# Moving eight later-modulation steps from the first linears of a transformer block to the linears beside its attention

## What is computed

```python
sh_l, sc_l, g_l = [m[:, None, :] for m in modulation(c, ada_w[i], ada_b[i])]
...
q_a = (rms_norm(c_q, q_lora_g) @ wq_b).reshape(b, l, A_HEADS, A_NOPE + A_ROPE)
kv_a = (rms_norm(c_kv, kv_lora_g) @ wkv_b).reshape(b, l, A_HEADS, A_NOPE + A_V)
...
lqp, lkp = apply_rope(lqp, ang_a), apply_rope(lkp, ang_a)
...
y_a = block_attention(lq_a, k_a_all, v_a_all, A_SCALE)
y_b = block_attention(lqb.reshape(b, s, B_KV_HEADS, B_GROUP, B_HEAD_DIM), k_b_all, v_b_all, B_SCALE)
```

## Time and profile before

| | us |
|---|---|
| median of 3 runs | 2868.02 (2866.8 to 2870.78) |
| profiled execution | 2862.45 |
| its span, first to last instruction | 2860.7 |
| TensorE matmuls busy | 2746.7 (96%) |
| VectorE busy | 1810.2 (63%) |
| ScalarE busy | 1247.6 (44%) |
| GpSimd busy | 271.8 (10%) |

### The profile page before, as it was taken

The page is one execution under the profiler, slowest core; times in us unless marked ns, Lnnn a source line. Parts: engine busy times, 40 slices in busy tenths (PEclk is TensorE's granted clock), DMA queues, the critical chain, the costliest instruction groups (busy, mean ns, idle before and its releaser), DMA issues.

```text
span 2860.7 us, 50571 instructions
## 1 busy us (share of the span) xinstructions
PE 2746.7 (96%) x22173; PEld 2595.9 (91%) x22173; DVE 1810.2 (63%) x2228; ACT 1247.6 (44%) x1375; POOL 271.8 (10%) x330
## 2 busy tenths in 40 slices
PE   6899999999999999999999999998999999999998
PEld 3598977788988998989999999988999999999998
DVE  2358867788777545556556556696566775467753
ACT  4333444445443344444444437545444444344444
POOL 0022102120111000002122120003000000000000
PEclk9899999999999999999999999999999999999999
DMA  9867535574776555435555553440245555555554
GB/s 375 323 228 259 192 135 193 209 274 171 252 246 228 192 193 176 163 137 188 179 175 175 176 177 138 156 166 16 104 171 196 193 188 191 198 196 195 194 189 140
DMA packets 93036, 546.88 MB, mean 191 GB/s; under 512 B 12657, under 2 KB 12817, under 8 KB 47889
## 3 DMA queue, kind: packets, MB, share of 16 engines
q1 hardware_dynamic: 69552, 466.39, 46.0%
q0 software_dynamic: 20480, 67.13, 7.0%
q10 hardware_dynamic: 2784, 10.15, 0.9%
HBM read 541.51 MB, written 2.10 MB: 190 GB/s over the span
## 4 chain that ended last, share of the span: by engine, by line
PE 67%; DVE 7%; ACT 2%; issue 2%; DMA 0%; DVEq 0%; ACTq 0%
PE bank L733 66%; DVE r L2173 2%; ACT r L1476 1%; DVE f L2743 1%; PE bank L801 1%; DVE f L2210 1%; DVE f L2807 0%; ACT f L1838 0%; DVE f L2804 0%; DVE f L2820 0%; DVE f L2796 0%; DMA f<-in_units 0%; DMA f<-in_later 0%; ACT L1826 0%; DVE f L2555 0%
## 5 line engine op out<-in xcount | busy, mean ns | idle before, releaser
L733 PE MATMUL bank<-r,r 128*128 128x256 f32 (+1 forms) x19596 | 2388.3, 284 | 40.5 <-DVE r L2173 18.3
L733 PEld LDWEIGHTS bank<-r,r 128*128 128x128 f32 x19596 | 2320.6, 189 | 98.8 <-DVE r L2173 25.9
L2173 DVE TENSOR_TENSOR r<-f,r 128x2048 fp32r<-128x2048 f32 (+2 forms) x447 | 961.3, 2152 | 687.2 <-ACT r L1476 685.0
L1476 ACT CAST r<-f 128x2048 fp32r<-128x2048 f32 (+2 forms) x447 | 792.0, 1774 | 850.3 <-PE bank L733 664.5
L733 PE MATMUL bank<-f,f 128*128 128x128 f32 (+9 forms) x1992 | 317.7, 375 | 51.5 <-DMA f<-in_units 23.0
L733 PEld LDWEIGHTS bank<-f,f 128*128 128x128 f32 (+2 forms) x1992 | 214.1, 175 | 111.7 <-issue 50.3
L2210 DVE SCALAR_TENSOR_TENSOR f<-f,f,f 128x512 f32<-128x512 f32 x240 | 179.8, 749 | 52.7 <-DMA f<-in_later 37.1
L3068 POOL DMA_DIRECT2D f<-in_later x256 | 137.5, 537 | 786.8 <-DVE f L2210 469.9
L2743 DVE SCALAR_TENSOR_TENSOR f<-f,f,f 128x255 f32<-128x255 f32 (+1 forms) x272 | 133.7, 494 | 8.8
L1493 ACT COPY f<-bank 128x512 f32<-128x512 f32 x149 | 83.9, 584 | 111.8 <-PE bank L733 106.1
L3077 POOL TENSOR_TENSOR f<-f,f 32x512 f32<-32x512 f32 x24 | 61.7, 2570 | 655.5 <-DVE f L2681 655.5
(11 more groups left out here) (236 smaller groups left out, 968.3 us busy)
## 6 DMA issues: line engine op xcount, KB each, us to landing
f<-in_units SPq DMA_DIRECT2D x346, 1024.0 KB, 4.8
f<-in_units SPq DMA_DIRECT2D x124, 768.0 KB, 4.3
f<-in_later POOLq DMA_DIRECT2D x256, 256.0 KB, 4.0
f<-in_units SPq DMA_DIRECT2D x8, 576.0 KB, 4.7
f<-in_x ACTq DMA_DIRECT2D x2, 1024.0 KB, 12.7
f<-in_ctx ACTq DMA_DIRECT2D x2, 1024.0 KB, 12.3
f<-in_x_turned ACTq DMA_DIRECT2D x1, 2048.0 KB, 13.4
out<-f SPq DMA_DIRECT2D x4, 256.0 KB, 4.2
```

The source lines that it names most:

```text
L733: return e.matmul(o, lhsT, rhs, start=start, stop=stop, skip_group_check=True)
L1476: e.copy(unit_view(high[HIGH_OF[u]][1], u), unit_view(raw[RAW_OF[u]][0], u)).then_inc(*up("w_hi", ("hi", u)))
L2173: e.tensor_tensor(unit_view(raw[RAW_OF[u]][1], u), unit_view(raw[RAW_OF[u]][0], u), unit_view(high[HIGH_OF[u]][1], u).bitcast(F32), ALU.su ...
```

## The change

Eight of the 96 steps that lie ahead of the Fourier layer are moved: five leave `kpe`, two leave `qb1`, one leaves the last gate block, and one is added to each of four first `wq` units and to each of four `wkv` units.

```diff
-LATER_STEPS_OF = {"ckv": (5, 5, 5, 5), "kpe": (3, 2, 2, 2), "qb1": (2, 1, 1, 1), "kb": (2, 1), ("gate", 2): (1, 1, 1, 1),
-                  ("gate", 0): (0, 0, 1, 1), ("gate", 1): (2, 1, 1, 1)}
-LATER_STEPS_OF.update({("wq", p): (2, 2) for p in range(4)})
-LATER_STEPS_OF.update({("wkv", p): (2,) for p in range(4)})
+LATER_STEPS_OF = {"ckv": (5, 5, 5, 5), "kpe": (1, 1, 1, 1), "qb1": (1, 1, 1, 0), "kb": (2, 1), ("gate", 2): (1, 1, 1, 1),
+                  ("gate", 0): (0, 0, 1, 1), ("gate", 1): (1, 1, 1, 1)}
+LATER_STEPS_OF.update({("wq", p): (3, 2) for p in range(4)})
+LATER_STEPS_OF.update({("wkv", p): (3,) for p in range(4)})
```

## The result

| | before | after |
|---|---|---|
| median of 4 runs each, us | 2867.41 (2866.55 to 2870.78) | 2899.55 (2895.29 to 2903.28) |
| profiled execution, us | 2862.45 | 2895.29 |
| its span, us | 2860.7 | 2893.5 |

The changed kernel is slower: ratio 1.012, 95% interval 1.0105 to 1.0136 (the quotient of the two medians in the table is 1.0112). The forecast of 2896 us was 3.6 us short of the median, and the range held it.

The account below looks back on a forecast made before the run. TensorE, busy in 96% of the span, was taken as the bound. Terms: -3.2 + 12.5 - 0.4 + 8.5 + 5.8 + 2.9 + 2 = +28.1 us, carried to the median 2868.0: 2896 us, range 2876 to 2908.

Parts of the forecast that it names:

- The gain: Ahead of units 54 and 55: both TensorE waits for low parts go, -3.2 us (between -2.5 and -3.4).
- The two waits that were to stay: Ahead of units 49 and 50: TensorE's waits of 1.42 and 2.90 us for low parts remain.
- Group 0: Units 74 to 78: late rotation, exponential and end's reduction delay the value product, +12.5 us (10.0 to 13.3).
- -0.4 for the end that leaves unit 79: At unit 79: an end no longer stands there, which saves 0.4 us.
- the prediction's own sign of being wrong: At unit 78: VectorE reaches the end before TensorE has finished the transposes of step 17; no size given.
- Group 1: Units 79 to 82: a late reduction of the end at 81 delays step 21's value product, +8.5 us (6.5 to 10).
- Groups 2 and 3: Units 82 to 86: late exponential of step 24 and late transposes at 539.43, together +5.8 us (4.7 to 6.3).
- Unit 86: Three steps in iteration 85 delay the low part that unit 86 needs, +2.9 us (2.4 to 4.5).
- The clock: After the new long TensorE waits, except the first: matmuls run at a lower clock, +2 us (0 to 5).
- Not slower: Rival, units 74 to 85: VectorE's idle time takes in the added steps, only -3.2 seen, 2865 us; chance 9%.
- The banks do not bite: Rival, units 74 to 86: ends find other banks free, only late VectorE work costs, +11.5, 2879.5 us; chance 14%.
- Loads slow each other: Rival, all triples of steps: moved loads take 5 us beside weight loads, +36 to +44, 2904 to 2912 us; 10%.

Follow-up runs that it names:

- e6_warm: Changed kernel with filler matmuls, their results unused, in TensorE's eight new waits: median 2892.07 us, ratio 1.0101 to the kernel before.
- e8_group0: Kernel before with one step more beside units 74 and 76, two fewer at the first kpe unit, end of block 5 at 78: 2877.08 us, 1.0044.
- e7_ends_79_82: Changed kernel with the ends of blocks 5 and 6 at units 79 and 82 instead of 78 and 81: median 2885.42 us, ratio 1.0066.
- e1_ends_apart: Changed kernel with the ends of blocks 5, 6 and 7 at units 79, 82 and 85 instead of 78, 81 and 84: median 2895.47 us, 1.0112.
- e5b_no_loads_before: Kernel before without the loads of the quarters of steps 40 to 71, all instructions kept: median 2863.64 us, ratio 1.0002.
- e2_ends_inside: Kernel before, own steps, with the ends of blocks 5, 6 and 7 at units 78, 81 and 84: median 2869.07 us, ratio 1.0017.
- e5_no_loads: Changed kernel without the loads of the quarters of steps 40 to 71, all instructions kept: median 2878.14 us, ratio 1.0048.
- e3_to_gates: Kernel before with five kpe and two qb1 steps put beside gate blocks 0 and 1 (units 66 to 73): median 2863.61 us, ratio 1.0003.

## Why the prediction was right, point by point

**The gain.** Forecast -3.2, measured -3.06 up to unit 74 and -3.3 in the means of all executions. The closeness of the one execution is luck, since single ones differ by more than that. Units 54 and 55 wait for nothing, as forecast. The stretch from 247.8 to unit 58 gave somewhat more than its term, and the longer wait ahead of unit 50 took it back. The two waits that were to stay have the forecast sum (4.27 against 4.32 us) but stand in one place. The code is the same up to there, and the loads landed otherwise: ahead of the low part of unit 49 VectorE waited 4.05 and 1.00 us for loads before, and 1.95 and 1.21 after; from there to the low part of unit 50 it waited 4.2 us before and 6.3 after.

**Group 0.** The prediction followed VectorE line by line on the clock of the trace before. Shifted by the 3.06 us, the trace after has the rotation done at 460.8 (forecast 461.1), the steps of iteration 76 at 468.9 (468.7), the maximum of step 16 at 472.4 (472.4), the scores of step 17 at 474.8 (474.6) and the value product at 480.08 (480.1). The waits for loads in iteration 76 were 3.5 us (1.04, 0.97 and 1.46) where the forecast's times leave 2.8; the rest of the chain fits within 0.3 us. The group lost 13.97 us and not 12.5, and the 1.5 between them are the value product at half clock. (The -0.4 for the end that leaves unit 79 belongs to group 1, since that end stood behind unit 79.)

One sign did not come as forecast. The value product was to wait 3 to 5 us for line 2226 and waited 0.21. By the letter, the prediction's own sign of being wrong appeared: VectorE was at the reduction of the end at 476.28, and TensorE was done with the transposes of step 17 at 476.80 (475.69 and 1.11). At full clock it would have been the other way round: the scores and transposes took 4.05 and 1.11 us in place of 2.07 and 0.66, and filled what would have been the wait. In e6_warm, with the clock up, the product does wait for that reduction, 1.66 us. So in this group the end's bank and the slow clock held the product until the same time, and the experiments say what the end was worth (7.6 us less with it at 79), not this wait.

**Group 1.** Forecast +8.5, less the 0.4 above. The terms that the prediction lists add up to 506.5 to 507.7 and not to 508.2 (it counts six quarters as 4.5 us, where four take 3.2), so by its own terms it is +6.8 to +8.0. The value product of step 21 came 7.9 us later within the group (518.52 - 499.75, less the 10.91 by which unit 79 was late), and 1.7 more came from it running at half clock (3.78 us, 1.89 before, of which 0.2 overlap with the next unit): +9.55 in all.

**Groups 2 and 3.** Forecast +5.8, measured +10.54. With the clock kept up, e6_warm, it is +6.5. The transposes of step 25 came 3.1 us later, 1.2 of them from the long unit's slow start and 1.9 from the wait, as forecast.

**Unit 86.** Forecast +2.9, measured +2.58. The wait for its loads was 0.96 us and not 1.45:

```profile
584.67 1.61 DVE L2210 SCALAR_TENSOR_TENSOR f<-f,f,f 128x512 f32<-128x512 f32 x2 [0.96 <-DMA f<-in_later]
586.20 3.69 DVE L2453 TENSOR_TENSOR r<-f,r 128x512 fp32r<-128x512 f32 x6
```

**The clock** is the term that was mis-sized: forecast +2, measured 6.9 in the profiles and 3.6 to 5.4 in the runs. The prediction put the slow matmuls of the first wait at nothing, since they would end before the bank is free, and they did. It passed over the value product behind them, which was slow as well. For the three other waits it took 2 us in all, less than the 1.3 us each that it had read from the earlier trace rows, where dense matmuls follow. Here short scores and transposes follow, with new waits between them, and the clock came back only with the next long unit. Without the clock's term the forecast for the four stretches is 12.5 + 8.1 + 5.8 + 2.9 = 29.3 us; e6_warm has 29.7 (11.9, 8.4, 6.5 and 3.0). That the totals are so close is in part luck, since each group is off by 0.1 to 0.7.

**The rivals.** "Not slower" is out by the wait of 2.47 us for the rotation, and e8_group0 shows the same with one group alone. "The banks do not bite" is out by e7_ends_79_82: had they not bitten, moving the ends would have brought nothing. "Loads slow each other" was right about the place and wrong about the size. The loads issued from 440 to 445 us and from 510 to 513 us of after took (issue to landing, as the earlier trace rows)

```profile
DMA to landing us min/median/max: 6.9/7.0/7.3
...
DMA to landing us min/median/max: 4.8/5.1/5.4
```

but elsewhere VectorE waited less for them than 5 us to landing would give: 1.09 and 0.51 us in iteration 79, and 0.96 ahead of unit 86. The span grew by 32.8 us, not by the 36 to 44 of this rival. The Trainium skill ("DMA: Bandwidth & Descriptors", the section on the anatomy of one DMA) gives a fixed cost and a rate by which such a load takes an estimated 2.6 us. The fastest load of before took 2.8 us and its median was 4.0; the measurement decides, and by the page's figure the waits for loads would have been forecast too short.

**Left open.** The medians differ by 32.1 us and the spans by 32.8, against a sum of 28.1. (The profiled execution missed its forecast by 4.7 us, 2895.29 against 2890.6, and the median by 3.6, because the 5.6 us carried from profile to median were 4.3 for the kernel after.) In the spans 4.9 is the clock's miss, and the small rest (0.4 in the stretches, 0.8 given back behind unit 86) was not followed. What the waits of e1_ends_apart in groups 2 and 3 owe to the moved end and what to the clock was not separated either.

## What to carry to other kernels

Follow the queue of the engine that gets the work, instruction by instruction, to the first thing that the bound engine wants from it: here 63% busy and 5 us of idle time beside units 79 and 82 did not help, because the idle time came after the want. Where banks go round in turn, a read-out that stands late in a queue costs as much as what it blocks; put it where its reader has time, and look at what stands behind it in the reader's queue. Behind the long units 79 and 82 it was cheap, since VectorE idles there anyway; behind 85 it held up the low part that unit 86 needs. Here steps were best taken from ahead of the work that TensorE already waits for (`ckv`), not merely from a stretch that has waits in it.

## What the runs showed of the hardware

- **A half clock outlasts the wait that caused it, but not every wait causes it.** In the kernel after, waits of 2.12, 3.02, 4.40 and 5.11 us inside the attention work were followed by matmuls at 0.50 to 0.63, in the longest case through 8.4 us of short attention work (471.70 to 480.10), until dense matmuls came. The wait of 2.88 us between two long runs of dense matmuls was followed by a clock of 1.00. Filling the waits brought 6.9 us of the 36.6 back in the profiles.
- **The same wait can end in either clock.** Behind a wait of 1.82 us in the gate blocks the value product took 1.98 us at 1.00 in before, after, e5b_no_loads_before, e6_warm and e7_ends_79_82, and 3.1 to 3.4 us in stretches at 0.64 to 0.69 in e1_ends_apart, e2_ends_inside and e5_no_loads, though none of these edits touches that place. Up to the 48 matmuls behind it this is worth 1.7 us.
- **The landing of the same loads differs between executions.** With the same steps up to there, the wait ahead of unit 50 was 4.27 us in the kernel after, 5.76 in e1_ends_apart, 5.30 in e5_no_loads, 6.17 in e6_warm, 2.56 in e7_ends_79_82 and 5.44 in e3_to_gates. With the steps of before it was 2.90, 2.95 (e2_ends_inside) and 5.13 (e5b_no_loads_before). Effects of 1 to 3 us at this place can't be read from one profiled execution, and the gain expected of e3_to_gates was of that size.
